# The second MLP's second product by seven quadrant products, with X updated from partial sums that go on adding up in PSUM

## The reference, cut to what matters

```python
h = _rms_norm(x, norm_mlp[i]) * (1.0 + sc2) + sh2
x = x + g2 * (jnp.square(jax.nn.relu(h @ mlp_w1[i])) @ mlp_w2[i])
```

## Time and profile before

| | |
|---|---|
| median of 3 runs | 2655.56 us (2654.34 to 2659.68) |
| the profiled execution's own time | 2655.41 us |
| its span, first to last instruction | 2653.6 us |
| PE busy | 2565.4 us, 97% of the span |
| DVE busy | 1352.0 us, 51% |
| ACT busy | 594.0 us, 22% |
| POOL busy | 545.2 us, 21% |
| mean granted clock of PE | 0.986 of full |

### The profile page before, as it was taken

How to read it: one execution, slowest core, us unless ns; L and a number is a source line. 1 busy time by engine, 2 the same in 40 slices (tenths; PEclk the granted TensorE clock), 3 DMA queues, 4 the chain that set the end, 5 groups by cost and what they waited for, 6 DMA issues and landing times.

```text
span 2653.6 us, 37530 instructions
## 1 busy us (share of the span) xinstructions
PE 2565.4 (97%) x14604; PEld 2243.7 (85%) x14604; DVE 1352.0 (51%) x2366; ACT 594.0 (22%) x982; POOL 545.2 (21%) x230
## 2 busy tenths in 40 slices
PE   7899999979999999999999999899999999999998
PEld 3878899968888888888888887788888888888887
DVE  6635752264384555555565555464444444444445
ACT  3311122142231121111121112651121111121112
POOL 6125321162122112112112111011121211212110
PEclk9999999989999999999999999899999999999999
DMA  7324523274211212211212111001010100101001
GB/s 236 147 69 144 161 96 112 104 268 152 72 48 64 71 55 66 85 55 57 69 55 81 69 55 32 24 26 39 32 47 32 47 32 32 47 32 47 32 32 80
DMA packets 126263, 199.48 MB, mean 75 GB/s; under 512 B 4420, under 2 KB 102504, under 8 KB 125800
## 3 DMA queue, kind: packets, MB, share of 16 engines
q1 hardware_dynamic: 123216, 188.76, 20.9%
q10 hardware_dynamic: 2968, 9.63, 1.2%
HBM read 167.44 MB, written 26.74 MB: 73 GB/s over the span
## 4 chain that ended last, share of the span: by engine, by line
PE 89%; DVE 5%; ACT 2%; DMA 2%; issue 2%; POOL 1%; ACTq 0%; SPq 0%; DVEq 0%; POOLq 0%
PE bank L314 83%; PE bank L1410 1%; PE bank L1563 1%; PE bank L1438 1%; DMA ada_st_in<-in_ada_w_dram 1%; PE bank L1475 1%; PE bank L1741 0%; DVE ada_acc_in L1059 0%; DMA SB<-state_spill 0%; DVE vtok L1113 0%; DVE xgm L1226 0%; POOL ringL L860 0%; DVE tL L1255 0%; ACT yn L686 0%; DVE h1L L1233 0%
## 5 line engine op out<-in xcount | busy, mean ns | idle before, releaser
L860 POOL TENSOR_TENSOR ringL<-stage,ringH 128x2048 fp32r<-128x2048 f32 x82 | 392.9, 4791 | 1829.1 <-ACT ringH L532 1829.1
L1067 DVE SCALAR_TENSOR_TENSOR X<-bank,mod,X 128x512 f32<-128x512 f32 (+1 forms) x792 | 515.2, 660 | 363.9 <-PE bank L314 359.6
L314 PE MATMUL bank<-midH,ringH 128*128 128x512 f32 (+1 forms) x1536 | 546.8, 356 | 3.3 <-DVE X L1067 3.3
L314 PE MATMUL bank<-midL,ringH 128*128 128x512 f32 (+1 forms) x1536 | 544.9, 355 | 0.0
L314 PE MATMUL bank<-midH,ringL 128*128 128x512 f32 (+1 forms) x1536 | 544.8, 355 | 0.0
L314 PE MATMUL bank<-hH,ringH 128*128 128x512 f32 (+1 forms) x1248 | 447.9, 359 | 0.2 <-DVE hL L1233 0.2
L314 PE MATMUL bank<-hH,ringL 128*128 128x512 f32 (+1 forms) x1248 | 443.2, 355 | 0.0
L314 PE MATMUL bank<-hL,ringH 128*128 128x512 f32 (+1 forms) x1248 | 443.0, 355 | 0.0
L1342 DVE TENSOR_TENSOR relu<-relu 128x512 f32<-128x512 f32 (+1 forms) x192 | 146.4, 763 | 568.9 <-ACT relu L774 568.7
L774 ACT ACTIVATE relu<-bank 128x512 f32<-128x512 f32 (+1 forms) x192 | 100.9, 527 | 1376.0 <-PE bank L314 1376.0
L314 PEld LDWEIGHTS bank<-midH,ringH 128*128 128x128 f32 x1536 | 291.5, 190 | 46.3 <-DVE X L1067 6.5
(11 more groups left out here) (191 smaller groups left out, 2894.0 us busy)
## 6 DMA issues: line engine op xcount, KB each, us to landing
stage<-in_mlp_w_dram SPq DMA_DIRECT2D x64, 1024.0 KB, 5.2
...
```

Source lines behind the costliest of these rows:

```text
L314: mm = nc.tensor.matmul(out, a, b, start=first and n == 0, stop=last and n == 2)
L860: nc.gpsimd.tensor_tensor(ringL[slot][:, :], stage[:, :], ringH[slot][:, :].bitcast(F32), ALU.subtract).then_inc(w_lo, 1)
L1067: V.scalar_tensor_tensor(out=X[:, d, cols(t)], in0=src[:, 0:TB[t][1]], scalar=gate_ap, in1=X[:, d, cols(t)], op0=ALU.mult, op1=ALU.add).th ...
```

## The change

The second product of chunks 1 to 14 of the second MLP is reshaped for the sample tokens. The weights of a chunk (256 hidden rows by 1024 outputs) are four quadrants: A11 and A12 are the outputs 0 to 511 from hidden tile 1 and 2, A21 and A22 the outputs 512 to 1023. The middle values are four quadrants too: B11 and B21 are hidden tiles 1 and 2 of the first 512 tokens, B12 and B22 those of the second 512. In place of eight products of quadrants there are seven, P1 to P7, of sums: S1 to S4 of the A (POOL, from `stage`) and T1 to T4 of the B (DVE). Each of the seven has four output tiles (d = 0 to 3) of one `pair_pass`, 3 matmuls. Sums of products that the scheme needs are formed in PSUM: P6 goes on adding in the bank of P1, P7 in that of P6, P4 in that of P7, P3 in that of P5. Every bank is evicted into X after each product, so that there are 28 evictions of 512 columns where there were 16; PE may add to a bank again once its eviction is done. P2, P3 and P5 use banks 6 and 7 in turn, the others banks 2 to 5. The prompt's 8 groups stay as they were, in other banks.

The square of the fourth middle tile (B22) and of the prompt's is made on ACT instead of DVE. The load of the final norm's row moves from before the chunks to the end of chunk 14, as its place is taken by T4.

```diff
@@ constants
+FACTORS = {1: ("A11", "B11"), 2: ("A12", "B21"), 3: ("S4", "B22"), 4: ("A22", "T4"), 5: ("S1", "T1"), 6: ("S2", "T2"),
+           7: ("S3", "T3")}
+GOES_TO = {1: (0, 0), 2: (0, 0), 6: (0, 1), 5: (1, 1), 7: (1, 1), 3: (0, 1), 4: (1, 0)}
+CHAIN = {6: 1, 7: 6, 4: 7, 3: 5}
+FAST_SEQ = ([(1, d) for d in range(HD)] + [(2, d) for d in range(HD)]
+            + [(p, d) for d0 in range(0, HD, 2) for p in (6, 5, 7, 3, 4) for d in (d0, d0 + 1)] + [("prompt", d) for d in range(DT)])
+FAST_BANK = [(2, 3, 6, 7, 4, 5, 2, 3)[d] if p == "prompt" else 6 + d % 2 if p in (2, 3, 5) else 2 + d for p, d in FAST_SEQ]
+LO_ORDER = ["B11", "B21", "T1", "T2", "T3", "B22", "T4", "p0", "p1"]
...
@@ SP
-        sp.wait_ge(a_mm, BATCHES_L0 + NCH)
-        sp.dma_start(fin[:, :], final_norm.rearrange("(o d) -> o d", o=1).to_broadcast([P, D])).then_inc(fin_in, 16)
...
+        sp.wait_ge(m2_mm[1], products(1, NCH - 1))
+        sp.dma_start(fin[:, :], final_norm.rearrange("(o d) -> o d", o=1).to_broadcast([P, D])).then_inc(fin_in, 16)
@@ ACT, mlp_fast
+            split_hi(U + 1, (m2_mm[1], products(1, ch)), (U_MLP[1] + 1) % 2)
+            act.wait_ge(s_add, 4 * ch)
+            nc.scalar.activation(sumH[:, :, :], sumF[:, :, :], ACT.Copy).then_inc(s_hi, 1)
+            relu(0, r_b[0][:, :])
...
+            high("T1")
+            relu(3, hidden("B22")[2])
+            square(3, hidden("B22")[2])
+            act.wait_ge(t_full, 4 * ch - 2)
+            high("T2")
...
+            relu(5, hidden("p1")[2])
+            square(5, hidden("p1")[2])
+            act.wait_ge(sqr_ok[1], n0 + 6)
+            high("p1")
+            split_hi(U + 2, (m1_mm[1], n0 + PAIRS), U_MLP[1] % 2)
@@ POOL, mlp_fast
+            pool.wait_ge(w_raw, 16 * (U + 2))
+            pool.wait_ge(m2_mm[1], products(1, ch) - DT)
+            nc.gpsimd.tensor_tensor(s1, a21, a22, ALU.add).then_inc(s_add, 1)
+            nc.gpsimd.tensor_tensor(s3, a11, a21, ALU.subtract).then_inc(s_add, 1)
+            pool.wait_ge(s_add, 4 * ch - 3)
+            nc.gpsimd.tensor_tensor(s2, s1, a11, ALU.subtract).then_inc(s_add, 1)
+            pool.wait_ge(s_add, 4 * ch - 1)
+            nc.gpsimd.tensor_tensor(s4, a12, s2, ALU.subtract).then_inc(s_add, 1)
+            split_lo(U + 1, (U_MLP[1] + 1) % 2)
+            pool.wait_ge(s_hi, ch)
+            nc.gpsimd.tensor_tensor(sumL[:, :, :], sumF[:, :, :], sumH[:, :, :].bitcast(F32), ALU.subtract).then_inc(s_lo, 1)
+            split_lo(U + 2, U_MLP[1] % 2)
@@ DVE, mlp_fast
+            def evict(n):
+                t, d = FAST_TILE[n]
+                own = earlier(FAST_TILE, n)
+                update(m2_mm[1], p0 + n + 1, m2_ev[1], bank[FAST_BANK[n]], mod[:, 1, 5 * DT + d, TB[t][2]:TB[t][2] + 1], t, d,
+                       (m2_ev[1], p0 + own + 1))
...
+            square(2)
+            dve.wait_ge(sqr_ok[1], n0 + 3)
+            V.tensor_tensor(t1, b12, b11, ALU.subtract).then_inc(t_full, 1)
+            for d in range(HD):
+                evict(d)
+            dve.wait_ge(sqr_ok[1], n0 + 4)
+            dve.wait_ge(t_full, 4 * ch - 3)
+            V.tensor_tensor(t2, b22, t1, ALU.subtract).then_inc(t_full, 1)
+            V.tensor_tensor(t3, b22, b12, ALU.subtract).then_inc(t_full, 1)
+            dve.wait_ge(t_full, 4 * ch - 2)
+            V.tensor_tensor(t4, b21, t2, ALU.subtract).then_inc(t_full, 1)
+            lower("T1")
+            dve.wait_ge(t_full, 4 * ch)
+            lower("T2")
+            evict(4)
+            evict(5)
+            lower("T3")
+            lower("B22")
+            evict(6)
+            evict(7)
+            lower("T4")
+            lower("p0")
+            lower("p1")
+            for n in range(2 * HD, FAST_GRP):
+                evict(n)
@@ PE, mlp_fast
+            def second_product(n):
+                p, d = FAST_SEQ[n]
+                w_name, m_name = FACTORS[p]
+                own = earlier(FAST_BANK, n)
+                pe.wait_ge(m2_ev[1], p0 + own + 1)
+                pe.wait_ge(mid_lo[1], h0 + LO_ORDER.index(m_name) + 1)
+                wH, wL = weight(w_name, d)
+                mH, mL, _ = hidden(m_name)
+                pair_pass(bank[FAST_BANK[n]][:, :], wH, wL, mH, mL, p not in CHAIN, True, chained=True).then_inc(m2_mm[1], 1)
...
+            pe.wait_ge(w_lo, UA + 1)
+            for g in range(3):
+                first_product(g)
+            pe.wait_ge(w_lo, UA + 2)
+            for d in range(HD):
+                second_product(d)
+            first_product(3)
+            for d in range(HD):
+                second_product(HD + d)
+            first_product(4)
+            first_product(5)
+            pe.wait_ge(s_lo, ch)
+            for n in range(2 * HD, 7 * HD):
+                second_product(n)
+            pe.wait_ge(mid_lo[1], h0 + FAST_MID)
+            for n in range(7 * HD, FAST_GRP):
+                prompt_product(n)
```

More of the change, by code:

```diff
@@ L98, with earlier, products, halves @@
 END_DVE_AT = {12: [0], 15: [1], 19: [2], 21: [3], 23: [4, 5, 6, 7, 8, 9]}
+FAST = [range(0, 0), range(1, NCH - 1)]
+HD = DT // 2
+FACTORS = {1: ("A11", "B11"), 2: ("A12", "B21"), 3: ("S4", "B22"), 4: ("A22", "T4"), 5: ("S1", "T1"), 6: ("S2", "T2"),
[4 more added lines that the diff above has]
+            + [(p, d) for d0 in range(0, HD, 2) for p in (6, 5, 7, 3, 4) for d in (d0, d0 + 1)] + [("prompt", d) for d in range(DT)])
+FAST_GRP = len(FAST_SEQ)
+FAST_BANK = [(2, 3, 6, 7, 4, 5, 2, 3)[d] if p == "prompt" else 6 + d % 2 if p in (2, 3, 5) else 2 + d for p, d in FAST_SEQ]
+FAST_TILE = [(2, d) if p == "prompt" else (GOES_TO[p][1], HD * GOES_TO[p][0] + d) for p, d in FAST_SEQ]
+LO_ORDER = ["B11", "B21", "T1", "T2", "T3", "B22", "T4", "p0", "p1"]
+FAST_MID = len(LO_ORDER)
+def earlier(seq, n):
+    return max([i for i in range(n) if seq[i] == seq[n]], default=-1)
+def products(l, ch):
+    if not isinstance(ch, int):
+        return FAST_GRP * ch + (GRP - FAST_GRP) if l == 1 else GRP * ch
+    return GRP * ch + (FAST_GRP - GRP) * sum(1 for c in FAST[l] if c < ch)
+def halves(l, ch):
+    if not isinstance(ch, int):
+        return FAST_MID * ch + (PAIRS - FAST_MID) if l == 1 else PAIRS * ch
+    return PAIRS * ch + (FAST_MID - PAIRS) * sum(1 for c in FAST[l] if c < ch)
 ADDS = {}
@@ L112, in advances_before @@
     return sum(1 for a in ADVANCE if a < s)
+END_NEED = [products(1, NCH - 1) + DT * (1 + (0 if n >= NS else 1 + n // 4)) for n in END_TILES]
 def after(eng, sem, n):
@@ L305, in cols, with pair_pass @@
         return slice(t0, t0 + w)
-    def pair_pass(out, w_hi_ap, w_lo_ap, m_hi_ap, m_lo_ap, first, last, weights_moving=False):
+    def pair_pass(out, w_hi_ap, w_lo_ap, m_hi_ap, m_lo_ap, first, last, weights_moving=False, chained=False):
         if weights_moving:
@@ L313, in pair_pass @@
         for n, (a, b) in enumerate(terms):
-            mm = nc.tensor.matmul(out, a, b, start=first and n == 0, stop=last and n == 2)
+            mm = nc.tensor.matmul(out, a, b, start=first and n == 0, stop=last and n == 2, skip_group_check=chained)
         return mm
@@ L348, in h_part, with hidden, weight @@
         return (hH, hL)[part][:, d, cols(tb)]
+    MID_PART = {"B11": (0, 0), "B21": (1, 0), "T1": (0, 1), "B22": (1, 1), "p0": (0, 2), "p1": (1, 2)}
+    def hidden(name):
+        if name in MID_PART:
+            k, tb = MID_PART[name]
+            return tuple(m[:, k, cols(tb)] for m in (midH, midL, midF))
+        i = int(name[1])
+        return tsH[i][:, :], tsL[i][:, :], tsF[i][:, :]
+    def weight(name, d):
+        if name[0] == "S":
+            i = int(name[1]) - 1
+            return tuple(m[:, i, d * P:(d + 1) * P] for m in (sumH, sumL))
+        k, n0 = int(name[2]) - 1, HD * (int(name[1]) - 1)
+        return tuple(r[(U_MLP[1] + 1) % 2][:, k * D + (n0 + d) * P:k * D + (n0 + d + 1) * P] for r in (ringH, ringL))
     def slot_free(U):
@@ L764, in hidden_hi @@
                 if g == 0:
-                    after(act, m2_mm[l], GRP * ch)
+                    after(act, m2_mm[l], products(l, ch))
                 tb = blocks[g // HT]
@@ L1363, in mlp, with mlp_fast, square, lower @@
                         finish(j)
+        def mlp_fast(ch):
+            n0, h0, p0 = PAIRS * ch, halves(1, ch), products(1, ch)
+            def square(g):
+                dve.wait_ge(relu_ok[1], n0 + g + 1)
+                V.tensor_tensor(r_b[g][:, :], r_b[g][:, :], r_b[g][:, :], ALU.mult).then_inc(sqr_ok[1], 1)
+            def lower(name, src=None):
+                hi, lo, full = hidden(name)
+                dve.wait_ge(mid_hi[1], h0 + LO_ORDER.index(name) + 1)
+                V.tensor_tensor(lo, full if src is None else src, hi.bitcast(F32), ALU.subtract).then_inc(mid_lo[1], 1)
+            def evict(n):
[3 more added lines that the diff above has]
+                       (m2_ev[1], p0 + own + 1))
+            b11, b21, b12 = (r[:, :] for r in r_b)
+            t1, t2, t3, t4, b22 = (hidden(name)[2] for name in ("T1", "T2", "T3", "T4", "B22"))
+            square(0)
+            lower("B11", b11)
```

(10 more changed lines are left out.)

80 lines of the change are left out of this document (70 added, 10 removed).

## The result

The changed kernel takes 2696.03 us (median of 4 runs, 2695.19 to 2696.52), the kernel before 2655.74 beside it. The ratio is 1.0146, with a 95% interval of 1.0134 to 1.0158: 40.3 us or 1.5% slower. I had forecast 2702.

The account below looks back on a forecast made before the run. PE was taken to bound the chunks. Terms of -2.7, +4.2, +0.15 and +1.7 us sum to +3.3 a chunk, +47 over 14, so 2655.4 becomes 2702 us, 1.7% slower; range 2672 to 2724, likeliest case 2690 to 2715.

Parts of the forecast that it names:

- (1): Sample's second product on PE: 84 matmuls instead of 96, -2.7 us a chunk.
- (2): PE's third product of P2 waits for DVE's eviction of (P2, d=0), behind five instructions: +4.2 us a chunk with restart.
- (3): At P7's start PE waits for DVE's eviction of (P6, d=0), behind the low half of p1: +0.15 us a chunk.
- (4): Behind the long P2 wait PE's clock falls to half for 3.4 us of running: +1.7 us a chunk.
- (5): POOL's four sums and extra split, ACT's copy and held low halves are covered within the chunk: nothing.
- E: Moment on PE when the fourth first-product group ends, right ahead of P2; the wait's chain is timed from it.
- the first of the five: First of DVE's T2, T3, T4, low T1, low T2 ahead of the needed eviction; forecast 0.61 us apart.
- A: Rival: the P2 wait without the clock's fall, +1.6 us a chunk, 2678 us; chance 0.12.
- B: Rival: DVE's evictions 0.75 us apart fall behind for the chunk's rest, +1.4 us a chunk, 2721 us; chance 0.09.
- C: Rival: DVE evicts in time, so the P2 wait doesn't form; 2620 us with no wait at all; chance 0.06.
- D: Rival: a partial P2 wait of 2.2 to 2.8 us, no clock fall, within 5 us of 2655; chance 0.03.

Follow-up runs that it names:

- e5: e4 with the evictions of (P6, d=0) and (P6, d=1) also moved ahead of the low half of p1 on DVE; 2616.01 us, ratio 0.9849.
- e3: Changed kernel with 16 unread matmuls into bank 0 between second and third product of P2, keeping PE busy through the wait; 2677.66 us, ratio 1.0082.
- e4: e1 with the fifth group of the first product put between the second and third product of P2 on PE; 2622.68 us, ratio 0.9874.
- e9: e5 with the low half of p1 moved eight evictions later instead of two, into POOL's split; 2631.53 us, ratio 0.9911.
- e10: e6 with the added DVE instruction behind the low half of p1 instead of ahead of it; 2635.23 us, ratio 0.9917.
- e6: e5 with one unread DVE instruction on 1536 columns added ahead of the low half of p1; 2720.59 us, ratio 1.0240.
- e1: Changed kernel with the evictions of (P2, d=0) and (P2, d=1) ahead of the wait for B22's square and the five DVE instructions; 2625.19 us, ratio 0.9887.
- e2: Changed kernel with the evictions of (P2, d=0) and (P2, d=1) behind two of the five DVE instructions instead of all five; 2656.86 us, ratio 1.0004.

## Why the prediction was right, by its steps

The mechanism was right, with each piece now measured apart. Terms per chunk:

| term | forecast | measured | from |
|---|---|---|---|
| (1) twelve matmuls fewer | -2.7 | -2.70 | e5 against before |
| (2) wait of (P2, d=2) and restart | +4.2 | +4.2 | what is left of the sum; directly 4.04 for the gap and 0.11 for the first matmul behind it (0.34 for 0.228, e3) |
| (3) P7 after P6 | +0.15 | +0.15 | e4 against e5 |
| (4) the clock's fall | +1.7 | +1.37 | changed kernel against e3 |
| (5) sums, splits, adding in PSUM, ACT's squares | 0 | 0 | e5: nothing left over of 2.70 |
| sum | +3.3 | +2.99 | 58.07 - 55.08 |

14 x 2.99 is 42 us, and the kernels differ by 40.3. In the profiled executions the second MLP starts 0.8 us earlier in the changed kernel, and what follows the last split of weights is 0.9 us shorter (71.02 for 71.95).

**The size that was off is term (4).** I let PE run 3.4 us at half the pace. The clock is at 0.50 for 3.4 us, but from the third chunk on the fall comes ahead of PE's return, so that PE runs about 3.0 us under it (2.96 in the rows above). What is lost is 0.25 us in the first matmul (0.59 to the next for 0.34), 1.0 in the five behind it (0.427 for 0.228) and 0.1 in the first of the prompt. 14 x 0.33 us is 4.6 of the 6 us between 2702 and 2696.

**That it falls in every chunk** was right, but rested on less than I thought. The idle times that I gave with the earlier trace rows are those of the windows; by the timeline PE was idle for 2.63 us where nothing fell, and for 2.92 and 6.35 where it did. And the kernel before had a shorter wait for an eviction, 2.26 us, with a fall, which I did not look at:

```profile
1619.14 0.58 PE L314 MATMUL bank<-midH,ringH 128*128 128x256 f32 x1 [2.26 <-DVE X L1067]
```
```profile
1619.10:1622.40 3.30, 3.26 (x15) 3.26 (x16) 1.94 (x5) 0.00 (x0) 3.30 (x1) 0.50 0.00 0
```

So the trace before already had waits of 2.26 us with a fall and of 2.63 without, and no limit between 2.4 and 2.5. At 4.04 us the fall came 14 times of 14.

**Term (2)** stands step by step: the square done at E + 1.46 for 1.53, the first of the five at E + 1.59 for 1.56, 0.60 apart for 0.61, the eviction at E + 4.61 as forecast, PE again at E + 5.40 for 5.51, since it follows the end of the eviction by less than the 0.15 that I took. The chain was read from rows of other stages, and they held. The second wait there, of (P2, d=3), is nothing, as said.

**What I said the profile would show:** a wait of 4.1 us in each chunk, ended by an eviction (3.9 by the profile, 4.04 over the pace); waits for X of some 60 us in 14 or 28 pieces (58.4, of which 54.4 in 14); chunks 58.5 apart (58.07). The mean clock was to fall by about 0.02; it fell by 0.008. My own working had 0.009 for the running part and put as much again on top for the idle part, which the rows do not show: the clock is at 1.00 through the wait up to its last 0.45 us.

**The rivals.** A (no fall) is e3, 2677.66 for 2678, and is not what the changed kernel does. B (DVE behind) is refuted: the 22 evictions of a chunk's end take 14.04 us, 0.63 apart and not 0.75, though each carries two waits; e9 and e10 show that DVE is 0.6 us from being this case. Nor does a fall last twice as long, as it does in every second chunk of e6. C, the faster side, needed DVE to take the evictions in time, and the order on DVE did not let it. With the order turned it comes at 2625.2 (e1), and at 2622.7 (e4) and 2616.0 (e5) with PE's list changed as well, where I had 2620. D is e2.

**What I missed** is a danger, not a term. I said that low halves beside POOL's splits can be held until about 12 us and are due later, which is so: that of B11 takes 4.32 us beside one and is done 12.2 us into the chunk. I did not see that a low half within 2 us ahead of a split stands in front of twenty evictions. The changed kernel passes that place by 1.4 us (low p1 ends at 1963.47, the split begins at 1964.91). e5, the fastest version, passes it by only 0.7 us (1946.88 and 1947.59), and 1.7 us more there cost e6 105 us over e5.
